# Scan block of a hybrid decoder step: five buffers for the new keys' rows, a later place for the sample probabilities, causal products on their own, and the last new states behind the opening split

## The reference, cut to what matters

```
def token_mixers(h, st_ssd, st_conv, st_gla, k_buf, v_buf, n_abs, keep, lp):
    ...
    y, ssd_new = ssd_chunked(xs, dt, A, bs..., cs..., st_ssd)
    ...
    att = dilated_attention(aq, k_ctx, v_ctx, k_buf.shape[1], n_abs)
    mix = jnp.concatenate([y, o, att], axis=-1) @ lp['w_out']

def ssd_chunked(x, dt, A, Bm, Cm, h0):
    cum = jnp.cumsum(dtc * A, axis=2)
    decay = jnp.exp(jnp.where(causal, cumT[..., :, None] - cumT[..., None, :], -jnp.inf))
    cb = jnp.einsum('bcqgn,bcsgn->bcgqs', Cc, Bc)
    y_diag = jnp.einsum('bcgrqs,bcsgrp->bcqgrp', cb[:, :, :, None] * decay, xdt)
    s_local = jnp.einsum('bcsgn,bcsgrp->bcgrpn', Bc, xdt * to_end[..., None])
    (h_last, h_in: a scan over the chunks, h = chunk_decay * h + s_local)
    y_off = jnp.einsum('bcqgn,bcgrpn->bcqgrp', Cc, h_in) * jnp.exp(cum)[..., None]
    return (y_diag + y_off), h_last
```

## Time and profile before

| | us |
|---|---|
| median of 3 runs (2701.70 to 2709.51) | 2702.33 |
| time of the profiled execution | 2703.0 |
| its span, first to last instruction | 2701.2 |
| scan block, layer 1: first and next block's first instruction | 780.95 to 909.23 |
| scan block, layer 2 | 2103.24 to 2227.45 |
| clock of TensorE over the span | 0.962 |

### The profile page before, as it was taken

The page is one execution under the profiler, slowest core; times in us unless marked ns, Lnnn a source line. Parts: engine busy times, 40 slices in busy tenths (PEclk is TensorE's granted clock), DMA queues, the critical chain, the costliest instruction groups (busy, mean ns, idle before and its releaser), DMA issues. The chain is left out here.

```text
span 2701.2 us, 48884 instructions
## 1 busy us (share of the span) xinstructions
PE 2581.1 (96%) x19043; PEld 2386.1 (88%) x19043; DVE 1665.0 (62%) x2860; ACT 1041.1 (39%) x1681; POOL 12.7 (0%) x43
## 2 busy tenths in 40 slices
PE   6999999899988999999999999999999889999998
PEld 4998998898866799999999999988978569999997
DVE  6772783655644678358578448547466437864864
ACT  4441452422442355235355325424135323542542
POOL 0000000000000000000000000000000000000000
PEclk8999999999997899999999999999999969999999
DMA  7346336411121223643332553553120313233332
GB/s 248 95 134 218 96 95 218 147 56 56 44 89 58 81 56 94 193 143 94 90 89 78 167 168 93 155 173 114 48 66 32 109 50 94 63 95 85 93 85 68
DMA packets 398241, 285.66 MB, mean 106 GB/s; under 512 B 18273, under 2 KB 396439, under 8 KB 397702
## 3 DMA queue, kind: packets, MB, share of 16 engines
q1 hardware_dynamic: 397676, 283.36, 34.7%
q10 hardware_dynamic: 410, 0.18, 0.0%
HBM read 271.71 MB, written 11.79 MB: 105 GB/s over the span
## 5 line engine op out<-in xcount | busy, mean ns | idle before, releaser
L347 PE MATMUL PS<-f_xH,f_wqH 128*128 128x288 f32 x2224 | 659.2, 296 | 3.1 <-issue 3.0
L347 PE MATMUL PS<-f_xL,f_wqH 128*128 128x288 f32 x2224 | 656.1, 295 | 0.0
L347 PE MATMUL PS<-f_xH,f_wqL 128*128 128x288 f32 x2224 | 654.0, 294 | 0.0
L347 PEld LDWEIGHTS PS<-f_xH,f_wqH 128*128 128x128 f32 x2224 | 416.7, 187 | 5.9 <-issue 5.4
L347 PEld LDWEIGHTS PS<-f_xH,f_wqL 128*128 128x128 f32 x2224 | 418.8, 188 | 0.0
L347 PEld LDWEIGHTS PS<-f_xL,f_wqH 128*128 128x128 f32 x2224 | 417.4, 188 | 0.0
L347 PE MATMUL PS<-f_actH,f_wqH 128*128 128x288 f32 x1408 | 323.8, 301 | 1.3 <-DVE f_wqL L964 1.3
L347 PE MATMUL PS<-f_actH,f_wqL 128*128 128x288 f32 x1408 | 315.3, 295 | 0.0
L347 PE MATMUL PS<-f_actL,f_wqH 128*128 128x288 f32 x1408 | 315.2, 295 | 0.0
L723 DVE SCALAR_TENSOR_TENSOR xT<-PS,modT,xT 128x288 f32<-128x288 f32 (+1 forms) x80 | 41.4, 517 | 366.0 <-PE PS L347 366.0
L347 PEld LDWEIGHTS PS<-f_actH,f_wqH 128*128 128x128 f32 x1408 | 230.1, 189 | 27.0 <-issue 25.0
(11 more groups left out here) (500 smaller groups left out, 4658.1 us busy)
## 6 DMA issues: line engine op xcount, KB each, us to landing
wslot<-in_ffn_w_in SPq DMA_DIRECT2D x176, 512.0 KB, 5.0
masks<-in_w_mod SPq DMA_DIRECT2D x42, 1536.0 KB, 6.8
wslot<-in_ffn_w_out SPq DMA_DIRECT2D x64, 384.0 KB, 4.1
wslot<-in_w_in SPq DMA_DIRECT2D x44, 512.0 KB, 4.7
wslot<-in_ffn_w_out SPq DMA_DIRECT2D x64, 320.0 KB, 3.3
setup<-in_w_mod SPq DMA_DIRECT2D x6, 1536.0 KB, 13.1
wslot<-in_w_out SPq DMA_DIRECT2D x16, 512.0 KB, 4.5
dec<-in_cache_attn_k SPq DMA_DIRECT2D x16, 384.0 KB, 3.8
```

Source lines behind the costliest of these rows:

```text
L347: ins = e.matmul(outs[j], w, x_hl[j][part], start=(start and w is wh and part == 0), stop=(stop and w is wl), skip_group_check=True)
```

## The change

Four things are edited, all in the scan block.

1. The rows of the new keys go to five places: two in `ktok` as before, three in the first three sample slots of `h0n`. VectorE's copies wait for no store; SP waits for all five stores before it loads the samples' states into `h0n`.
2. In steps 1 and 3 TensorE's `segments(k + 1)` moves from ahead of the cached keys to behind the first of the step's two samples. In step 7 `segments(8)` moves from ahead of the values to behind those of sample 0.
3. The causal product becomes a function of its own, `causal(k)`. Those of steps 5 and 6 are done earlier, behind `parts` of the step before (that of step 5 ahead of the negated scores). The minimum of the scores moves to step 5. The sample probabilities (exponentials, division, turning, copying) move from step 5 to step 6, behind the samples' first scores of decay and `steps`. `turn_h0(0)` and `turn_h0(1)` follow them, and `outputs(2)` gets a wait for `cbm_ready`.
4. At the end the sum of squares of the last piece comes first, then two new states, the opening split (`out_lo` and two mixed tiles), and then the last two new states.

```
+            def key_rows(t):
+                return ktok[:, t, :] if t < 2 else h0n[:, t - 2].rearrange("p j n -> p (j n)")
...
-                        e.dma_start(dst, ktok[0:P if t < NCH else TS, t % 2, :]).then_inc(sem(f"k_stored{t % 2}"), 16)
+                        e.dma_start(dst, key_rows(t)[0:P if t < NCH else TS]).then_inc(sem("k_stored"), 16)
...
+                    e.wait_ge(sem("k_stored"), 16 * NTT)
                     for b in range(NB):
                         e.dma_start(h0n[:, b], A["state_ssd"][bass.ds(l, 1), b]
...
-                    e.wait_ge(sem("k_stored0"), 16 * 3)
-                    e.wait_ge(sem("k_stored1"), 16 * 2)
...
+                        if 2 * p + 1 == NKB + 1:
+                            e.wait_ge(sem("cbm_ready"), 2 * p + 3)
...
-                        if g == 1 and k + 1 < NK:
+                        if k == NKB + 1:
                             segments(k + 1)
-                        if k == NKB + 1:
-                            for j in range(NJ):
-                                turn_p(j)
                         for b in KEYS_AT[k] if k < NKB else ():
                             turn_keys(b)
                             if b >= 1:
                                 scores(b - 1)
+                            if g == 1 and b == KEYS_AT[k][0]:
+                                segments(k + 1)
...
-                        if k == NKB + 2:
-                            turn_h0(0)
-                            turn_h0(1)
...
                             values(b)
+                            if k == NK - 3 and b == 0:
+                                segments(k + 1)
                         if k == NK - 2:
                             new_states(0)
+                        if k == NKB + 2:
+                            segments(k + 1)
                         if g == 0 and p + 1 < NP_:
                             turn_x(p + 1)
-                        if g == 0:
+                        if g == 0 and k != NKB + 2:
                             segments(k + 1)
+                        if k == NKB + 2:
+                            for j in range(NJ):
+                                turn_p(j)
+                            turn_h0(0)
+                            turn_h0(1)
...
-                        if k == NKB + 1:
+                        if k == NKB + 2:
                             for j in range(NJ):
                                 e.wait_ge(sem("dec_neg_max"), 1)
...
+                    def causal(k):
+                        ...
+                        e.wait_ge(sem("seg_done"), k + 1)
+                        if k >= 2:
+                            e.wait_ge(sem("ssd_parts"), k - 1)
+                        e.tensor_tensor(cbm[0:n, g, 0:n], PS[0:n, 6, R3 * P:R3 * P + n],
+                                        tri[:] if c < NCH else tri8[:], ALU.mult).then_inc(sem("cbm_ready"), 1)
...
-                        if t >= 2:
-                            e.wait_ge(sem(f"k_stored{t % 2}"), 16 * (t // 2))
-                        e.tensor_copy(ktok[0:nt, t % 2, :], PS[0:nt, t % 2, 0:AI]).then_inc(sem("ktok_kept"), 1)
+                        e.tensor_copy(key_rows(t)[0:nt], PS[0:nt, t % 2, 0:AI]).then_inc(sem("ktok_kept"), 1)
...
-                        if g == 0 and p + 1 < NP_:
+                        if g == 0 and p + 1 < NP_ and k != NKB + 2:
                             steps(p + 1)
+                        if k not in (NKB + 1, NKB + 2):
+                            causal(k)
                         parts(k)
+                        if k == NKB + 2:
+                            steps(p + 1)
...
                         if k == NKB:
+                            times_dt(p + 1)
+                            causal(k + 1)
                             e.wait_ge(sem("dec_scored"), 1)
...
+                        if k == NKB + 1:
+                            causal(k + 1)
                             e.wait_ge(sem("dec_neg"), 2)
                             e.tensor_reduce(nmaxd, Sd[:], AX.X, ALU.min).then_inc(sem("dec_neg_max"), 1)
-                        if k == NKB + 1:
+                        if k == NKB + 2:
                             e.wait_ge(sem("dec_exps"), NJ)
...
-                    for b in range(NB // 2, NB):
+                    sum_squares_of(NP_ - 1)
+                    for b in range(NB // 2, NB // 2 + 2):
                         new_state(b)
-                        if b == NB // 2:
-                            sum_squares_of(NP_ - 1)
                     out_lo(e, u_out)
                     ...
+                    for b in range(NB // 2 + 2, NB):
+                        new_state(b)
```

More of the change, by code:

```diff
@@ L2908, in _ @@
                     y_root(0)
-                    for t in range(2):
-                        e.wait_ge(sem(f"k_stored{t}"), 16 * (3 - t))
+                    e.wait_ge(sem("k_stored"), 16 * NTT)
                     e.wait_ge(sem("rows_stored"), 32)
@@ L2947, in times_dt @@
                                         bc(dt_[0:n, c * SH:(c + 1) * SH], 2, SP_), ALU.mult).then_inc(sem("xdt_ready"), 1)
+                    def causal(k):
+                        p, g = divmod(k, 2)
+                        c = ORD[p]
+                        _, n = tok(c)
+                        e.wait_ge(sem("seg_done"), k + 1)
[3 more added lines that the diff above has]
+                                        tri[:] if c < NCH else tri8[:], ALU.mult).then_inc(sem("cbm_ready"), 1)
                     def parts(k):
@@ L2955, in parts @@
                         half = slice(g * R3 * SP_, (g + 1) * R3 * SP_)
-                        e.wait_ge(sem("seg_done"), k + 1)
-                        e.tensor_tensor(cbm[0:n, g, 0:n], PS[0:n, 6, R3 * P:R3 * P + n],
-                                        tri[:] if c < NCH else tri8[:], ALU.mult).then_inc(sem("cbm_ready"), 1)
                         e.wait_ge(sem("ssd_exps"), k + 1)
@@ L3070, in _ @@
                                     .then_inc(sem("dec_pt_kept"), 1)
-                        if g == 0 and p + 1 < NP_:
+                        if g == 0 and p + 1 < NP_ and k != NKB:
                             times_dt(p + 1)
```

## The result

| device us, median (range) | before, same chip | changed | ratio, 95% interval |
|---|---|---|---|
| changed kernel, 5 runs | 2707.76 (2701.70 to 2710.78) | 2690.27 (2687.34 to 2695.38) | 0.9942 [0.9922, 0.9962] |

The change makes the kernel 0.58% faster, 15.7 us by the ratio and 17.5 by the two medians, where 18.5 were forecast. The forecast time of 2684 started from a median of 2702.33; on the chip of this comparison the kernel before has 2707.76, and that accounts for most of the 6 us between 2684 and 2690.27. The execution that was profiled is the slowest of the five, 2695.38 us with a span of 2693.4, against 2703.0 and 2701.2 before. These two spans differ by 7.8 us only. The two scan blocks alone are 17.2 us shorter; 4.4 us are lost ahead of the first, 4.7 between the two and 0.4 behind the second, in code that is the same.

What follows compares the result with a forecast made beforehand. TensorE, busy 2581.1 of 2701.2 us, was taken to bound the kernel. Gains of 10.0 us in layer 1 and 8.5 in layer 2, together 18.5, gave 2683.8 against the median 2702.33, stated as 2684; range 2674 to 2694.

Steps and rivals of the forecast that it cites:

- Opening: Block start to end of `segments(1)`: store wait goes and clock stays up; gain 5.8 us layer 1, 5.3 layer 2.
- Steps 1 and 3: TensorE's 1.18 us wait for ScalarE's exponentials is covered in each step: 4.7 us in all, bounds 0 and 4.7.
- Steps 4 to 7, idle times: TensorE's 6.0 us of idle time becomes five shorter waits summing to 5.75: 0.25 us gained a layer.
- Steps 4 to 7, clock: Shorter idle times let `segments(6)` and `outputs(2)` run at 2.4 GHz: 2.0 us a layer, bounds 0 and 7.4.
- if the clock falls before `outputs(2)`: One of the signs named in advance that would show the prediction wrong, in steps 4 to 7.
- Values: Order unchanged, but layer 2's fast last values may be lost: 1.0 us charged, between 0 and 3.1.
- End: Block end: SP's last issues come behind VectorE's last states; 0.4 us lost in each layer, bounds 0 and 0.8.
- Rival 3: Steps 5 to 7: VectorE becomes the bound, three new waits grow 1.8 us each; about 2695 us, chance 0.10.
- Rival 4: Clock falls in the opening and stays at 1.2 GHz through steps 1 to 3; 2711 us and up, chance 0.03.
- Rival 2: Clock falls as before, in opening and steps 4 to 7; gain 11.3 us, about 2691, chance 0.17.
- Rival 1: Clock holds through steps 6 and 7 or rises in the values; 2674 to 2680 us, chance 0.12.

Runs made afterwards that it cites:

- kernel with fills in steps 5 and 6: Changed kernel plus nine products that nobody reads, placed where TensorE waits in steps 5 and 6; 2676.37 us, ratio 0.9895.
- the fillers: Nine unread products in steps 5 and 6, in the changed kernel (2676.37 us) and again with all last new states ahead of the split (2674.23 us).
- middle-alone kernel: Kernel before with only the third edit (new order of causal products and sample probabilities) and `segments(8)` behind sample 0's values; 2708.92 us, ratio 1.0007.

## Why the prediction was right, point by point

- **Opening.** Forecast 5.8 and 5.3 us; measured 17.22 - 11.39 = 5.83 and 16.65 - 11.39 = 5.26, and the five places alone give the same. Wait and clock were both sized right, against this one profile of the kernel before; in the other profiles with two buffers the opening took 16.4 to 19.0 us. The clock stayed at 1.00 from there to step 5.
- **Steps 1 and 3.** Forecast 2.4 a layer, measured 25.76 - 23.02 = 2.74. It is a little more than the wait of 2.36, so the upper bound of 4.7 for both layers was too low against 5.5. But on top of the five places it made the blocks no shorter: the values ran at a lower clock, 2.76 us longer, and no difference in the time can be told. The prediction looked for a wait that is late next, and did not price this.
- **Steps 4 to 7, idle times.** Forecast 1.2, 0.5, 1.6, 1.7 and 0.75; measured 1.18, 0.47, 1.71, 0.28 and 0.71. Four of five hold, and the idle time went down by 1.65 us a layer, where 0.25 were forecast. The fourth had been counted with TensorE at full speed; at 1.2 GHz its own work ahead of the probabilities covers most of VectorE's. That is time moved from idle to busy, no gain. In the kernel with fills in steps 5 and 6, where this stretch is fast, 1.65 us lie between the end of the next piece's rows (833.97) and the first probabilities (835.62), part of them filled: VectorE's 1.7 was right.
- **Steps 4 to 7, clock.** This is the step that failed by layers. I took 2.0 us in each, and layer 1 lost 0.28 in the whole part while layer 2 won 4.67. With 1.65 us of idle time gone in each, TensorE's products took 1.9 us longer in layer 1 and 3.0 us less in layer 2. That the mean of the part, 2.2, meets the 2.25 of the forecast is luck: of the six blocks with this order and no fill only this one came near 29. The reason given, that shorter idle times keep the clock up, is refuted as the mechanism: with the idle times of the change the clock in layer 1 fell ahead of `outputs(2)`, sooner than before. And the five places alone, with the long idle times of 2.40 and 2.76 us left in, won 2.2 and 2.5 us in this part, in layer 1 more than the whole change. Only the fillers, which leave about 1.7 us of idle time where the change leaves 4.35, held it: in three of four blocks up to the first values, and in the fourth but for the short fall shown above. The forecast said it would be wrong "if the clock falls before `outputs(2)`", and in layer 1 it was.
- **Values.** I charged 1.0 us for the luck of layer 2, so this term was sized too small; it cost 42.90 - 40.16 = 2.74, near the bound of 3.1. Layer 1 won 0.18.
- **End.** Forecast 0.4 lost in each layer, measured 0.68 and 0.52, and 0.74 for the edit alone. SP was last, as expected, and the next block started 1.5 us behind VectorE, not 1.2. The direction, that this edit alone is a loss, is shown in the marks, while the total can't tell it.
- **Sum.** Opening 11.1, steps 1 to 4 5.5, steps 4 to 7 4.4, values -2.6, end -1.2: 17.2 us in the two blocks, where 18.5 were forecast by 11.1, 4.8, 4.5, -1.0 and -0.8. The sum was close because the opening, its greatest term, held and the errors in the values (1.6) and the steps (0.7) partly met; the third term was right only in the mean of two blocks. By the ratio the time went down 15.7, with an interval of 10 to 21 us.
- **The rivals.** Rival 3, VectorE as the bound, fell: the idle times are not longer than worked out. Rival 4 fell: 1.00 from the opening to step 5. Rival 2 held for steps 4 to 7 of layer 1 alone, not for the opening. Rival 1 did not come by the change; with the nine fillers it did, and a time of 2676.37 lies in the 2674 to 2680 that it gave. The Trainium skill, "TensorE: Matmul & The Clock Gate", Part 4, has transposes not count for TensorE's clock. That would make the change lose its opening term; here 43.7 us with the transposes of the cached keys among them ran at 1.00, so this trace speaks against a strict reading. No run here has transposes alone for so long: where the clock held through the turned probabilities in the kernels with fills, other products stand around them.

## What to carry to other kernels

Where TensorE bounds and its granted clock has two levels, an idle time costs its own length and can have a slow stretch behind it, whose place can shift: read the granted clock beside the idle times, compare block by block and in more than one profile, and do not add up the gains of edits before both have run together. If TensorE's short waits cannot be taken away, unread products in them can be worth far more than a reordering (here 14 us against nothing measurable); where there was no idle time they cost what they gave back. Moving an engine's work behind its part of the split pays only if nobody else, SP's issues here, then becomes the last at the barrier.

## What the runs showed of the hardware that was not expected

- The clock's slow time in layer 1 was 64.5 us before and 64.8 after the change, at other places, although 5.9 us of waits net had gone ahead of it (3.76 and 2.36, less 0.21 that the wait for ScalarE's first copy grew). I had taken it to shrink with them.
- Code that is the same took 1194.01 us between the two blocks before, 1198.70 in the changed kernel, and 1190.96 to 1196.75 in the others. A single span can thus mislead by more than most edits here are worth.
- TensorE's wait behind the first store was 4.07 to 5.54 us in the kernels with two buffers, while the 0.32 in its place was the same in every kernel with five places. Part of what the edit takes away is this spread; for example, the block of the middle-alone kernel in layer 2 was 5.8 us longer than before, 2.4 of that in the opening.
- What stays open: why the clock falls ahead of `outputs(2)` in layer 1 and within it in layer 2 with equal idle times, and how much of the 6.5 us that the five places alone won behind step 4 another run would keep.
